# Layer norm sums of a diffusion backbone: Pool's partial sums against sums taken wholly on TensorE

## What is computed

```python
def layernorm(x, g, b):
    xf = x.astype(F32)
    mu = jnp.mean(xf, axis=-1, keepdims=True)
    var = jnp.mean(jnp.square(xf - mu), axis=-1, keepdims=True)
    return ((xf - mu) * lax.rsqrt(var + LN_EPS) * g + b).astype(x.dtype)

def half_ffn(x, shift, scale, gate, w_in, w_out, g, b):
    h = modulate(x, shift, scale)
    a, u = jnp.split(h @ w_in, 2, axis=-1)
    y = (jax.nn.silu(a) * u) @ w_out
    return layernorm(ALPHA * x + 0.5 * gate * y, g, b)

# per layer: x = half_ffn(x); x = layernorm(ALPHA*x + gate*mixer(x)); x = half_ffn(x)
# layer 0: mixer = Hyena long convolution and RG-LRU; layer 1: latent attention, latent tokens only from there
```

## Time and profile before

| what | value |
|---|---|
| median of 3 runs | 2861.99 us |
| lowest, highest | 2858.74, 2862.37 us |
| profiled execution, its own time | 2864.44 us |
| its span, first to last instruction | 2862.8 us |
| TensorE busy | 2805.3 us, 98% of the span |
| DVE, ACT, POOL busy | 1995.5, 1024.5, 315.6 us |
| mean granted TensorE clock | 0.997 |

### The profile page before, as it was taken

The page is one execution under the profiler, slowest core; times in us unless marked ns, Lnnn a source line. Parts: engine busy times, 40 slices in busy tenths (PEclk is TensorE's granted clock), DMA queues, the critical chain, the costliest instruction groups (busy, mean ns, idle before and its releaser), DMA issues.

```text
span 2862.8 us, 46110 instructions
## 1 busy us (share of the span) xinstructions
PE 2805.3 (98%) x17194; PEld 2449.2 (86%) x17194; DVE 1995.5 (70%) x3239; ACT 1024.5 (36%) x1613; POOL 315.6 (11%) x411
## 2 busy tenths in 40 slices
PE   7999999999999999999999999999999999999999
PEld 3888999988867888989998899999978998878888
DVE  5776777766766676776677877777676887554555
ACT  3322232346631422322225233332265665521221
POOL 1101000111100000010010000000204654100000
PEclk9999999999999999999999999999999999999999
DMA  9434432222132244344421222222310101233331
GB/s 341 153 118 163 131 96 66 73 60 63 56 118 59 68 148 153 125 151 142 154 67 45 67 67 66 66 66 66 98 42 23 27 21 45 81 104 103 95 95 60
DMA packets 302274, 267.74 MB, mean 94 GB/s; under 512 B 30662, under 2 KB 257866, under 8 KB 302026
## 3 DMA queue, kind: packets, MB, share of 16 engines
q1 hardware_dynamic: 279530, 186.93, 22.0%
q0 software_dynamic: 21760, 76.03, 7.5%
q10 hardware_dynamic: 864, 3.15, 0.3%
HBM read 260.83 MB, written 5.24 MB: 93 GB/s over the span
## 4 chain that ended last, share of the span: by engine, by line
PE 91%; DVE 4%; DMA 2%; ACT 1%; issue 1%; POOL 0%; SPq 0%; POOLq 0%; DVEq 0%; ACTq 0%
PE PSALL L2997 15%; PE PSALL L2998 15%; PE PSALL L2999 15%; PE PSALL L3315 8%; PE PSALL L3316 8%; PE PSALL L3317 8%; PE PSALL L3073 2%; PE PSALL L2918 2%; PE PSALL L3075 2%; PE PSALL L3074 2%; PE PSALL L3743 2%; PE PSALL L3728 1%; PE PSALL L3026 1%; PE PSALL L3608 1%; PE PSALL L3586 1%
## 5 line engine op out<-in xcount | busy, mean ns | idle before, releaser
L2087 DVE SCALAR_TENSOR_TENSOR X<-PSALL,GATE,X 128x512 f32<-128x512 f32 x480 | 280.5, 613 | 107.3 <-PE PSALL L2999 106.7
L3315 PE MATMUL PSALL<-HHI,WSH 128*128 128x384 f32 x816 | 275.2, 337 | 4.1 <-DVE U L2112 2.8
L3316 PE MATMUL PSALL<-HLO,WSH 128*128 128x384 f32 x816 | 274.0, 336 | 0.0
L3317 PE MATMUL PSALL<-HHI,WSL 128*128 128x384 f32 x816 | 273.7, 335 | 0.0
L2997 PE MATMUL PSALL<-GHIA,WHIW 128*128 128x512 f32 (+1 forms) x618 | 217.4, 352 | 12.7 <-DVE X L2087 7.7
L2998 PE MATMUL PSALL<-GLOA,WHIW 128*128 128x512 f32 (+1 forms) x618 | 213.2, 345 | 0.0
L2999 PE MATMUL PSALL<-GHIA,WLOW 128*128 128x512 f32 (+1 forms) x618 | 212.6, 344 | 0.0
L2997 PE MATMUL PSALL<-GHIB,WHIW 128*128 128x512 f32 (+1 forms) x618 | 212.4, 344 | 0.0
L2999 PE MATMUL PSALL<-GHIB,WLOW 128*128 128x512 f32 (+1 forms) x618 | 212.3, 344 | 0.0
L2998 PE MATMUL PSALL<-GLOB,WHIW 128*128 128x512 f32 (+1 forms) x618 | 212.2, 343 | 0.0
L1222 ACT ACTIVATE WSH<-RAW 128x512 fp32r<-128x512 f32 x204 | 129.1, 633 | 231.4 <-DVE RAW L2164 159.7
(11 more groups left out here) (435 smaller groups left out, 6986.3 us busy)
## 6 DMA issues: line engine op xcount, KB each, us to landing
RAW<-in_ffn_w_in_dram SPq DMA_DIRECT2D x176, 512.0 KB, 4.1
ADA<-in_ada_w_dram POOLq DMA_DIRECT2D x128, 512.0 KB, 5.7
RAW<-in_ffn_w_out_dram SPq DMA_DIRECT2D x88, 512.0 KB, 3.8
RAW<-in_ev_w_in_dram SPq DMA_DIRECT2D x20, 512.0 KB, 4.2
ADAF<-in_ada_w_dram POOLq DMA_DIRECT2D x16, 512.0 KB, 10.6
WRAW<-in_mla_w_q_up_dram SPq DMA_DIRECT2D x16, 288.0 KB, 3.0
RAW<-in_ev_w_out_dram SPq DMA_DIRECT2D x8, 512.0 KB, 4.3
RAW<-in_mla_w_in_dram SPq DMA_DIRECT2D x8, 512.0 KB, 4.3
```

What stands on the lines that cost most here:

```text
L2087: dve.scalar_tensor_tensor(X[:, m, lo:lo + n], down_bank(m, s, 2), GATE[:, j, m, s:s + 1], X[:, m, lo:lo + n], ALU.mult, ALU.add).then_inc ...
L3315: te.matmul(out, w_hi, hi[block](k), start=(k == 0), stop=False)
L3316: te.matmul(out, w_hi, low[block](k), start=False, stop=False)
L3317: x = te.matmul(out, w_lo, hi[block](k), start=False, stop=(k == 3))
```

## The change

Pool's additions go: `X_ADDED`, `adds`, `add_chunks`, `last_sums` and the semaphore `ln_add` are removed, with all calls. `sums` on TensorE takes all eight chunks straight from X, chunk 0 like the others behind its eviction. Nothing is moved; the groups of sums stand where they stood and are longer.

```diff
-X_ADDED = {1: 5, 0: 4}
...
-        def add_chunks(name, S, a, evicted):
-
-            lo, n, _ = part(name, a)
-            total, (count, done) = RSTD[:, lo:lo + n], adds(name, a)
-            for m in range(1, count + 1):
-                pool.wait_ge(evac, evicted(a, m))
-                if m > 1:
-                    pool.wait_ge(ln_add, done + m - 1)
-                pool.tensor_tensor(total, X[:, 0, lo:lo + n] if m == 1 else total, X[:, m, lo:lo + n],
-                                   ALU.add).then_inc(ln_add, 1)
...
-        last_sums("ln0", "ffn0")
...
-        for a in range(2):
-            add_chunks("ln4", 1, a, lambda a, m: plan["mla_out"].evac + m + 1)
-        for a in range(2):
-            add_chunks("final", 1, a, lambda a, m: last_evac("ffn3", 1, a, m))
...
-        def sum_chunks(name, a):
-
-            return [0] + list(range(adds(name, a)[0] + 1, KC))
-
         def sums(name, S, a, evicted, ms=None):
 
             lo, n, _ = part(name, a)
-            count, done = adds(name, a)
-            for m in sum_chunks(name, a) if ms is None else ms:
-                te.wait_ge(*((ln_add, done + count) if m == 0 else (evac, evicted(m))))
+            for m in range(KC) if ms is None else ms:
+                te.wait_ge(evac, evicted(m))
                 if m == 0 and a == 1 and SUM_BANKS[name][0] == SUM_BANKS[name][1]:
                     te.wait_ge(ln_std, plan[name].ln + 1)
-                src = RSTD[:, lo:lo + n] if m == 0 else X[:, m, lo:lo + n]
+                src = X[:, m, lo:lo + n]
...
-                sums(then, 2, 1, lambda m: e0 + KC + m + 1, sum_chunks(then, 1)[:-1])
+                sums(then, 2, 1, lambda m: e0 + KC + m + 1, range(KC - 1))
...
-            sums("ln1", 2, 1, latent, (0, 4, 5))
+            sums("ln1", 2, 1, latent, range(6))
...
-            sums("ln4", 2, 1, evicted(1), sum_chunks("ln4", 1)[:-1])
+            sums("ln4", 2, 1, evicted(1), range(KC - 1))
```

More of the change, by code:

```diff
@@ L372, in build @@
     evac = sem("evac")
-    ln_add, ln_sum, ln_var, ln_mu, ln_mean, ln_cen, ln_sq, ln_std, ln_rstd, ln_root, ln_n, ln_h32, ln_x = (
-        sem(f"ln_{n}") for n in ("add", "sum", "var", "mu", "mean", "cen", "sq", "std", "rstd", "root", "n", "h32", "x"))
+    ln_sum, ln_var, ln_mu, ln_mean, ln_cen, ln_sq, ln_std, ln_rstd, ln_root, ln_n, ln_h32, ln_x = (
+        sem(f"ln_{n}") for n in ("sum", "var", "mu", "mean", "cen", "sq", "std", "rstd", "root", "n", "h32", "x"))
     flt_in, tab_in, kf_out = sem("flt_in"), sem("tab_in"), [sem(f"kf_out{n}") for n in range(2)]
@@ L615, in build @@
                  "ln3": last_evac("ffn2", 2, 1, KC - 1), "ln4": plan["mla_out"].evac + 12}
-    def adds(name, a):
-        return X_ADDED[part(name, a)[2]] - 1, sum(X_ADDED[part(n, b)[2]] - 1 for n in LN_PARTS for b in range(parts_of(n))
-                                                  if n != "h0" and plan[n].ln + b < plan[name].ln + a)
     def quarter(name, a):
@@ L933, in _ @@
                         .then_inc(bd_in[n % 2], 16)
-        out_evac = lambda a, m: plan["ev_out"].evac + (8 if m < 4 else m + (5 if a == 0 else 9))
-        add_chunks("ln1", 2, 0, out_evac)
-        add_chunks("ln1", 2, 1, out_evac)
         pool.wait_ge(evac, plan["ln1"].evac)
@@ L942, in _ @@
         rebuild("ffn1")
-        last_sums("ln2", "ffn1")
         rebuild("ffn2")
-        last_sums("ln3", "ffn2")
         def swap_parts(h, t):
```

## The result

The changed kernel takes 2869.29 us at the median of 15 runs (2865.95 to 2872.29), the kernel before 2861.99 us (15 runs, 2856.94 to 2864.96). The ratio is 1.0027, 95% interval 1.0019 to 1.0034: 7.7 us slower by the ratio, with 5.4 to 9.7 as its interval. Two later measurements of the same kernel against the kernel before gave 1.0026 (1.0016 to 1.0037) and 1.0024 (1.0014 to 1.0033). The forecast was 2868.1 us, 6.1 us slower, in a range of 2863.5 to 2872.0; the measured time lies inside.

What follows compares the result with a forecast made beforehand. The prediction took TensorE, busy 98% of the span, to bound the kernel. Added chunks of 6.40 us less 0.3 us for an earlier load gave 6.1 us, so 2861.99 + 6.1 = 2868.1 us, range 2863.5 to 2872.0.

Steps and rivals of the forecast that it cites:

- The price of the added chunks: At the norms' sums: 0.11 us per chunk over 64 tokens, 0.22 over 128, 0.43 for PART; 6.40 us on the path.
- What is hidden: Part 1 of `ln4` hides 0.34 us behind TensorE's 1.02 us wait; `ln0`, `ln2` and `ln3` hide nothing.
- ACT's row with its 0.36 us: In `ln0`, ACT waits 0.36 us for the latent sums before scaling the mean, so its queue starts later with them.
- What Pool gives back: Before `ln4`, without Pool's addition, a weight load is issued 0.53 us earlier and lands earlier: 0.3 us gained.
- the pair: DVE's two weight-tile subtractions before `ln4`: 2.88 us beside a Pool addition, 2.35 without.
- the second load: Before `ln4`, the load issued once the pair frees its tile: 6.40 us long, to be issued 0.53 us earlier.
- the credit: The 0.3 us taken off the 6.40 for the load before `ln4` landing earlier; it may be nothing or 0.5.
- Absorption: Rival: waits after the latent sums of `ln0`, `ln2`, `ln3` hide 1.6 us, giving 2866.5 us; chance 0.15.
- the lone-chunk price: Rival: each added chunk costs 0.36 us over 128 tokens, 0.25 over 64; net 10.8 us, 2872.8; chance 0.08.
- the faster kernel: Rival: all 40 Pool additions held up DVE by 0.53 us each; net 14.8 us faster, 2847; chance 0.03.
- the sums cost nothing: Rival: TensorE takes the added sums in gaps elsewhere and only the credit is left, 2861.7 us; chance 0.04.

Runs made afterwards that it cites:

- The kernel with doubled chunks: The changed kernel with every chunk of the sums taken twice, scales halved: 2884.98 us, ratio 1.0079 against the kernel before.
- the busy Pool: The changed kernel with Pool's 40 additions left in and two more per addition, results unused: 2869.38 us, ratio 1.0023 against the kernel before.

## Why the prediction was right

**The bound.** TensorE is the chain, and none of its waits was for Pool's sums. Right: no such wait went with the additions, and with 120 additions beside the norms the kernel is not measurably slower than the changed one.

**The price of the added chunks.** Right in each term, to the 0.01 us of the rows: 0.45, 0.33, 0.22 and 0.43. Taking the price from the steps between groups of different length, not from a group's mean or a lone chunk, made it so, and the eight-chunk group of the squares was the same work at its final length. The kernel with doubled chunks shows the same steps, and the lags of four traces of the changed kernel show that all of it, 6.4 us, stays.

**What is hidden.** Right at part 1 of `ln4` (1.02 to 0.68), and right that `ln0`, `ln2` and `ln3` hide nothing although TensorE waits there as well. Both places look alike in the list of waits; ACT's row with its 0.36 us tells them apart. In part 1 of `ln4` the low part comes over a way that does not pass the sums. One row was misread on the way: TensorE's 0.29 us at 626.61 ends with DVE's low part of 626.14 to 626.56, not with the one at 623.60. Since ACT works without a pause from its wait of 0.36 us to that low part, the reading stands.

**What Pool gives back.** Here the mechanism holds only in part, and that the size of "I take 0.3" is near the 0.2 us worked out from the six traces is luck. Its first half came true: the pair is at 2.35, and the second load goes out 0.54 us earlier against the first. But what follows, that TensorE's start hangs on the second load, holds in two of fourteen traces, the one that the forecast read (0.41 us) and one more (0.08); in the others the first load alone sets the wait, or there is none, and the first load's issue does not move. The statement that the other additions meet a subtraction only "where TensorE has its input already" is wrong in the very trace that was read: the one at 2446.44 was stretched by 0.38 us and ended TensorE's wait of 0.90. Where the second load is not late, that row is all that Pool costs. Nothing of this can be seen in a total or in the mean of the waits (1.37 us without the addition, 1.20 with it, each row spreading over almost 2 us), so a gain of 0.3 us is neither shown nor excluded by them. One trace was read as if a DMA's time were a property of the place. Without the credit the forecast would have been 6.40, nearer to the measured ones.

**The total.** 6.40 against 7.7 (5.4 to 9.7), 7.4 and 6.9 us by the three ratios. The middle values lie about 1 us above the sum; the intervals hold it. If a small term is missing, it is not at the norms, where four traces add up to 6.4; among the waits and clock falls elsewhere, which differ from execution to execution, it can't be told. The chances of 0.50 slower and 0.47 same were drawn around 6.1 against a limit of 5.7 us. That the changed kernel is slower is clear (1.0019 at least). Its middle value is over that limit too, but its interval begins just under it, so the call of slower came true by a narrow margin.

**The rivals.** Absorption is refuted by ACT's rows and by the lags, which do not fall back behind the sums, not even with the chunks doubled; the lone-chunk price by the groups of 1.03 and 1.67; the faster kernel by the result and by the busy Pool; and that the sums cost nothing by the result.

## What to carry to other kernels

A reduction that an idle engine does for free is not free to take back: each chunk on the bounding engine is paid in full wherever the chain passes it, and its price is the step between a short and a long group of the same rows. To see whether a wait behind added work will absorb it, ask who releases the wait and whether that engine, in its own order, waits for the work itself. A gain that rests on one DMA landing earlier needs more than one trace, and in each of them the question which of the loads ended the wait.

## What had not been expected of the hardware

- One DMA load of 512 KB at the same place of the same kernel took 4.05, 5.21 and 5.76 us from issue to use; over fourteen traces, with small changes to the kernel, 3.76 to 5.76. TensorE's waits behind it ran from 0 to 2.03 us, in step with it.
- The granted clock of TensorE falls from 2.4 to 1.2 GHz for a short stretch, mostly right behind a wait of 1 to 3 us, at partly other places in each execution; one such stretch cost the changed kernel 1.5 us at 1085 us and another 1.4 us at 2524 us. Behind the waits before `ln4` it fell in four of the fourteen traces (after waits of 1.75 to 2.00 us; in one of them the granted clock is 0.76 from 2451 to 2458 us), which cost about 1.5 us more, but not after the longest, 2.03 us, in the changed kernel (1.00 from 2449 to 2456).
- Pool's additions lengthen DVE operations with two SBUF inputs (1.22 to 1.66, 1.75 and once 2.31 us, 0.42 to 0.93 and once 1.08), and 85 operations with one SBUF input lost under 0.2 us together; even so, the total with 108 us of such Pool work shows no cost of it.
